# Neighbourhood attention in steps of two heads, and gated-linear units with both head parities together, on one core of a Trainium2

## The chip, the cores and the metric

The kernel runs on one core of a Trainium2 chip. The metric is the device time of one execution in microseconds (us), the median of several runs. The core has five engines, each with its own instruction queue: TensorE (PE, matrix products; PEld is its weight load), VectorE (DVE), ScalarE (ACT), GpSimd (POOL) and SyncE (SP), which issues most DMAs. They wait for each other through semaphores alone.

## What is computed

The reference runs two blocks of two layers each on 512 tokens of width 1024, in fp32. The first block mixes tokens by pooling and latent attention in layer 0 and by neighbourhood attention in layer 1, each followed by cross attention to 256 memory tokens and a squared-ReLU MLP. The second block, on the 512 tokens and 256 context tokens, mixes them by four heads of retention and four heads of gated linear attention (GLA), followed by an MLP. The two parts that matter here:

```python
def neighbourhood_attention(q, k, v, rpb):   # 16 heads of 64, grid of 8 rows x 64 columns
    def one_row(args):
        k_win = k_rows[:, :, col_idx]        # a window of 8 rows x 16 columns for each query
        s = jnp.einsum('bchd,brckhd->bhcrk', q_row, k_win) * scale
        s = s + bias
        p = jax.nn.softmax(s.reshape(B, H, GRID_W, kh * kw), axis=-1)
        return jnp.einsum('bhcrk,brckhd->bchd', p, v_win)

def chunked_gated_linear_attention(q, k, v, log_a, s0, strict):   # chunks of 64 tokens
    def step(s, blk):
        q_dec, k_inv, k_end = qc * exp(cum), kc * exp(-cum), kc * exp(cum_last - cum)
        scores = where(mask, einsum('bhtd,bhsd->bhts', q_dec, k_inv), 0.0)
        o = einsum('bhts,bhsv->bhtv', scores, vc) + einsum('bhtd,bhdv->bhtv', q_dec, s)
        s_new = exp(cum_last[..., 0, :])[..., :, None] * s + einsum('bhsd,bhsv->bhdv', k_end, vc)
```

GLA runs in two directions (d = 0 forward, d = 1 backward), each over 12 chunks (4 of context, 8 of tokens).

## The kernel before

The program is written as one function per engine (`tensor`, `scalar`, `vector`, `gpsimd`, `sync`) that walks through all stages in the order of that engine's queue. A label names the result of an instruction (`then_inc`), and `wait_ge` on the label makes another engine wait for it. All orders are written out by hand. All instructions go through small helpers, so most TensorE rows of the profile carry line 94 (matmul) or 97 (transpose), ScalarE's line 100, and VectorE's lines 107 to 134.

Large projections use split fp32 operands (three products a term, type fp32r). The parts below use plain fp32 operands; each such product stands in the trace as two records, each transpose as one.

**Neighbourhood stage** (TensorE: `neighbour_scores`, `neighbour_transposes`, `neighbour_values`, lines 1060 to 1108; ScalarE: lines 1799 to 1819; VectorE: `divide`, lines 2545 to 2572; GpSimd: line 2967 on). The queries are permuted to blocks of 128 that see 256 keys. For head h the stage has four query blocks q. Two heads share the 128 partitions of O1.Q and O1.K: head h lies on partitions 64 x (h % 2) on, so a score product contracts over 64 rows of the array (form 64*128 in the rows), always the same half within a head. VectorE adds the bias table (O1.BE, made by GpSimd from a DMA of the relative bias and a mask) and takes the least value (line 131), ScalarE takes the exp with its sum, VectorE divides (reciprocal, line 134, and a scaling, line 111), TensorE transposes the 128 x 256 probabilities by halves into banks 2, 3 and 7 in turn, and ScalarE copies a whole head's transposes (two copies of 512 columns, O1.PT). The value products have 64 columns of weights (form 128*64), written to 64 partitions of bank 4 or 5 by the head's parity. ScalarE copies them out ("oh") and VectorE writes the low part ("ol") for the output projection. The loop runs over heads: scores of head h + 1 by blocks, between them the transposes of head h, and after the second block's scores all value products of head h - 1. Scores use banks 0, 1 and 6 in turn.

**GLA units.** `mixed_units` interleaves retention tasks with GLA units. A "work" unit (d, y) stands for a pair of chunks i and a parity par of heads: heads 2j + par, j = 0, 1. There are 12 a direction in layer 0 and 8 in layer 1, 40 in all. On TensorE a unit has `inside` of the next unit (KI by QD: two products that contract over the 64 rows of parity par, form 64*128, 128 columns), then the products of the carried states H.STT with QD (four, 64 rows, 64 columns), then the masked inside scores H.GS with the values H.GV (two full products), all into one bank ("gout"). VectorE's `clip` (line 124) copies the inside scores under a mask into one of two buffers H.GS. The outputs of direction 0 are copied by ScalarE (`first_outputs`), those of direction 1 added by VectorE (`gather`) and multiplied with the gate (`gated`). `gla_banks` hands out banks 4 to 7 in turn, in the order in which the units use them. `states` writes the carried states, state 0 being zeros from a memset.

## Time and profile before

| what | value |
|---|---|
| median of 3 runs | 3515.75 us (3507.23 to 3529.01) |
| the profiled execution, own time | 3525.86 us |
| its span, mean granted TensorE clock | 3524.1 us, 0.979 |
| TensorE busy | 3398.9 us, 96% |
| VectorE, ScalarE, GpSimd busy | 56%, 37%, 7% |
| neighbourhood stage | 975.3 to about 1087 us |
| GLA and retention, layer 0 and layer 1 | about 1960 to 2085, and 2990 to 3090 us |

The profile gives the busy time of each engine, the chain of work that ended last (at each step what released the instruction), groups of instructions by line and shape, and the granted clock of TensorE, where 1.00 is 2.4 GHz and 0.50 is 1.2 GHz. Busy time of TensorE overlaps between neighbouring records, since they are pipelined: how far apart two starts are tells more than a duration.

### The profile page before, as it was taken

Reading aid. Unit: us, or ns where it says so; the run is one execution under the profiler, and the core shown is the slowest. Engines: PE = TensorE matmul, PEld = TensorE weight load, DVE = VectorE, ACT = ScalarE, POOL = GpSimd, SP = SyncE. Lnnn points to the kernel's source line nnn. Section 1 sums busy time; section 2 is a strip of 40 time slices with the busy share of each in tenths; the row PEclk is TensorE's granted clock in tenths of the full one; section 3 lists DMA queues with packets and bytes.
Section 4 is the critical chain, followed back from the end, with each engine's and each line's share of the span. In section 5 each row is a group of like instructions: output and inputs, shape, how many; then the busy total and the mean of one; then the engine's idle time right before and its main releaser. Section 6 shows DMA issues by size and latency. Waiting matters only on the chain.

```text
span 3524.1 us, 41864 instructions
## 1 busy us (share of the span) xinstructions
PE 3398.9 (96%) x17160; PEld 2706.5 (77%) x17160; DVE 1964.9 (56%) x3491; ACT 1320.8 (37%) x2311; POOL 233.9 (7%) x319
## 2 busy tenths in 40 slices
PE   7989999999989999999999889999999999899999
PEld 6747677777867677777898567888888887568887
DVE  6464578886654568887214675333334326664434
ACT  5353434345353444344212443333233313343332
POOL 1200000001041010000000001000001000000000
PEclk9999999999999999999999899999999999899999
DMA  5302145442202135543311021211112321123222
GB/s 177 107 14 84 48 156 167 168 156 90 87 22 70 44 124 171 176 166 118 127 60 49 14 78 41 72 60 60 60 60 67 128 72 42 42 64 102 88 94 72
DMA packets 210181, 317.19 MB, mean 90 GB/s; under 512 B 5377, under 2 KB 154499, under 8 KB 208709
## 3 DMA queue, kind: packets, MB, share of 16 engines
q1 hardware_dynamic: 194180, 243.20, 21.4%
q0 software_dynamic: 15808, 71.31, 5.9%
q8 instruction: 135, 2.21, 0.3%
q14 instruction: 58, 0.47, 0.0%
HBM read 300.76 MB, written 14.59 MB: 89 GB/s over the span
## 4 chain that ended last, share of the span: by engine, by line
PE 84%; DVE 10%; ACT 5%; issue 1%; DMA 1%; ACTq 0%; SPq 0%; DVEq 0%
PE ps L94 83%; ACT t L100 5%; DVE t L115 4%; DVE t L107 3%; PE ps L97 1%; DVE t L111 0%; DVE t L121 0%; DVE t L131 0%; DVE ps L115 0%; DMA t<-in_ada_w 0%; DMA t<-in_w_in 0%; DVE ps L107 0%; DMA t<-in_mem 0%; ACT L100 0%; DVE ps L112 0%
## 5 line engine op out<-in xcount | busy, mean ns | idle before, releaser
L94 PE MATMUL ps<-t,t 128*128 128x512 f32 (+6 forms) x16736 | 3348.5, 365 | 98.0 <-DVE t L115 43.0
L94 PEld LDWEIGHTS ps<-t,t 128*128 128x128 f32 (+3 forms) x16736 | 2657.8, 189 | 761.8 <-issue 150.8
L100 ACT ACTIVATE t<-t 128x1024 fp32r<-128x1024 f32 (+6 forms) x1210 | 846.1, 734 | 1031.3 <-PE ps L94 796.3
L107 DVE TENSOR_TENSOR t<-t,t 128x1024 fp32r<-128x1024 f32 (+4 forms) x799 | 734.2, 953 | 625.3 <-ACT t L100 621.3
L100 ACT ACTIVATE t<-ps 128x512 f32<-128x512 f32 (+6 forms) x552 | 270.7, 517 | 784.4 <-PE ps L94 760.4
L115 DVE SCALAR_TENSOR_TENSOR t<-t,t,t 128x256 f32<-128x256 f32 (+2 forms) x919 | 433.8, 534 | 17.8 <-ACT t L100 11.3
L107 DVE TENSOR_TENSOR t<-ps,t 128x512 f32<-128x512 f32 (+5 forms) x317 | 195.1, 638 | 215.8 <-PE ps L94 147.2
L115 DVE SCALAR_TENSOR_TENSOR t<-ps,t,t 128x512 f32<-128x512 f32 (+2 forms) x252 | 155.0, 662 | 243.5 <-PE ps L94 223.3
L107 POOL TENSOR_TENSOR t<-t,t 128x64 f32<-128x64 f32 (+2 forms) x213 | 150.5, 730 | 1699.3 <-ACT t L100 1695.7
L100 ACT ACTIVATE t<-t,t 128x256 f32<-128x256 f32 (+4 forms) x272 | 144.3, 554 | 214.7 <-DVE t L107 149.7
L118 DVE COPY t<-ps 128x512 f32<-128x512 f32 (+3 forms) x100 | 47.2, 510 | 221.4 <-PE ps L94 208.3
L115 DVE SCALAR_TENSOR_TENSOR t<-ps,t 128x512 f32<-128x512 f32 (+1 forms) x155 | 94.4, 617 | 46.1 <-ACT t L100 24.7
L100 ACT ACTIVATE t<-ps,t 128x256 f32<-128x256 f32 (+3 forms) x92 | 49.5, 546 | 129.4 <-PE ps L94 97.0
L97 PE MATMUL ps<-t,t 128*128 128x128 f32 (+1 forms) x424 | 72.5, 295 | 19.1 <-DMA t<-in_mem 8.1
L97 PEld LDWEIGHTS ps<-t,t 128*128 128x128 f32 (+1 forms) x424 | 51.4, 149 | 47.5 <-issue 14.1
L140 POOL DMA_DIRECT2D t<-in_ada_w x48 | 42.7, 889 | 624.2 <-DVE t L115 624.2
L111 DVE TENSOR_SCALAR t<-t,t 128x256 f32<-128x256 f32 (+3 forms) x173 | 71.7, 418 | 5.9
L121 DVE TENSOR_REDUCE t<-ps 128x1 f32<-128x512 f32 (+1 forms) x64 | 35.4, 553 | 16.2 <-PE ps L94 15.9
L140 POOL DMA_DIRECT2D t<-gates_away x10 | 5.9, 592 | 535.1 <-PE ps L94 506.0
L115 DVE SCALAR_TENSOR_TENSOR t<-t,t,ps 128x128 f32<-128x128 f32 (+1 forms) x96 | 36.2, 380 | 7.0 <-PE ps L94 4.4
L124 DVE COPY_PREDICATED t<-t,ps 128x256 f32<-128x256 int32 x40 | 17.7, 442 | 39.6 <-PE ps L94 39.0
L115 DVE SCALAR_TENSOR_TENSOR ps<-t,ps 128x512 f32<-128x512 f32 (+2 forms) x43 | 27.3, 634 | 19.5 <-ACT t L100 17.5
(36 smaller groups left out, 275.8 us busy)
## 6 DMA issues: line engine op xcount, KB each, us to landing
t<-in_w_ff SPq DMA_DIRECT2D x64, 1024.0 KB, 5.2
t<-in_w_mlp SPq DMA_DIRECT2D x64, 1024.0 KB, 5.3
t<-in_ada_w POOLq DMA_DIRECT2D x48, 1024.0 KB, 5.9
t<-in_w_in SPq DMA_DIRECT2D x30, 1024.0 KB, 5.3
t<-in_w_qkv_o SPq DMA_DIRECT2D x12, 1024.0 KB, 5.1
t<-in_w_mem_kv SPq DMA_DIRECT2D x8, 1024.0 KB, 6.3
t<-in_w_mem_q SPq DMA_DIRECT2D x8, 1024.0 KB, 4.9
t<-in_w_mem_o SPq DMA_DIRECT2D x8, 1024.0 KB, 5.0
```

Of the source, the lines that this page charges most:

```text
L94: return Issued(self, self.e and self.e.matmul(o, l, r, start=start, stop=stop, skip_group_check=True))
L97: return Issued(self, self.e and self.e.transpose(o, i, ident))
L100: return Issued(self, self.e and self.e.activation(o, i, f, **kw))
L107: return Issued(self, self.e and self.e.tensor_tensor(o, a, b, op))
L111: return Issued(self, self.e and self.e.tensor_scalar(o, a, s1, None, op0))
L115: return Issued(self, self.e and self.e.scalar_tensor_tensor(out=o, in0=a, scalar=s1, in1=b, op0=op0, op1=op1))
L118: return Issued(self, self.e and self.e.tensor_copy(o, a))
L121: return Issued(self, self.e and self.e.tensor_reduce(o, a, AX, ALU.max))
L124: return Issued(self, self.e and self.e.copy_predicated(o, mask.bitcast(mybir.dt.int32), a))
L140: return Transfer(self, self.e and self.e.dma_start(dst, src))
```

## The change

**Neighbourhood stage.** The loop runs over 32 steps s; step s is the pair of heads 2j, 2j + 1 with j = s // 4, and block q = s % 4. In each step TensorE issues the scores of both heads, which lie on different row halves, alternately and into different banks (0 and 1, or 6 and 7 in the next step), then the values of step s - 3 and the transposes of step s - 2 (four of them, in one bank, 2 or 3). The value products of both heads go to the two partition halves of one bank (4 or 5 by j), alternately. ScalarE takes two exps, one copy of 512 columns for the four transposes, and copies a pair of heads out at once (128 partitions instead of 64). VectorE has two adds, one reciprocal for both heads, two scalings, and the low part for a pair. O1.SB and O1.PT become four smaller buffers each, O1.BE four buffers instead of two, and the sums lie in a new tile STB (on the space of ST4). GpSimd makes the tables of the heads up to 3 without a wait, and later ones after the last block of the pair before.

**GLA units.** `inside` now issues both parities of a chunk pair, alternating, in even units and two units ahead; `outputs` issues the state products of both parities, alternating, in odd units, followed by the masked products of both. H.GS has four buffers. State 0 is left out: its products are skipped, and the first state is a copy. ScalarE's `first_outputs` and VectorE's `clip`, `gather` and `gated` follow in pairs. In layer 1 pending `states` also run ahead of an "end" unit of retention.

The diff, cut to its core:

```diff
-        for h in range(-1, 17):
-            for q in range(4):
-                if h + 1 < 16:
-                    neighbour_scores(h + 1, q)
-                if h > 0 and q == 1:
-                    neighbour_values(h - 1)
-                if 0 <= h < 16 and q > 0:
-                    neighbour_transposes(h, q - 1)
-            if 0 <= h < 16:
-                neighbour_transposes(h, 3)
+        for s in range(35):
+            if s < 32:
+                neighbour_scores(s)
+            if s >= 3:
+                neighbour_values(s - 3)
+            if 2 <= s < 34:
+                neighbour_transposes(s - 2)
...
+        def neighbour_scores(s):
+            j, q = s // 4, s % 4
...
+            windows = [(0, 256, 128 * q)] if q < 3 else [(0, 128, 384), (128, 128, 0)]
+            for x, (o0, n, t0) in enumerate(windows):
+                for a in range(2):
+                    bk, r0 = score_banks[s % 2][a], 64 * a
+                    if x == 0:
+                        opening(bk)
+                    ins = pe.matmul(P[bk][:, o0:o0 + n], O1.Q[r0:r0 + 64, j, 128 * q:128 * q + 128], O1.K[r0:r0 + 64, j, t0:t0 + n],
+                                    x == 0, x == len(windows) - 1)
...
+        def neighbour_values(s):
...
+            pe.wait_ge("pt", "na", s)
+            for c0, t0, n in [(0, 128 * q + 64, 128)] if q < 3 else [(0, 448, 64), (64, 0, 64)]:
+                for z in range(2):
+                    for a in range(2):
+                        h = 2 * j + a
+                        ins = pe.matmul(P[bk][64 * a:64 * a + 64, t0:t0 + n], O1.V[:, (q + z) % 4, 64 * h:64 * h + 64],
+                                        O1.PT[s % 4][:, 2 * a + z, c0:c0 + n], q == 0 and z == 0, t0 == 0 and z == 1)
...
         def inside(d, y):
-            i, par = work[d][y]
-            b0, bk = 64 * par, gb["inside", d, y]
-            opening(bk)
+            i = work[d][y][0]
+            bks = [gb["inside", d, y + par] for par in range(2)]
+            for bk in bks:
+                opening(bk)
             for j in range(2):
                 pe.wait_ge("qd", l, d, j)
                 pe.wait_ge("ki", l, d, j)
-                ins = pe.matmul(P[bk][:, 128 * j:128 * j + 128], H.KI[b0:b0 + 64, j, 128 * i:128 * i + 128],
-                                H.QD[b0:b0 + 64, j, 128 * i:128 * i + 128], True, True)
+                for par in range(2):
+                    b0 = 64 * par
+                    ins = pe.matmul(P[bks[par]][:, 128 * j:128 * j + 128], H.KI[b0:b0 + 64, j, 128 * i:128 * i + 128],
+                                    H.QD[b0:b0 + 64, j, 128 * i:128 * i + 128], True, True)
...
+        def outputs(d, y):
+            i, order = work[d][y][0], chunk_order(d)
+            obs = [gb["gout", d, y + par] for par in range(2)]
+            for ob in obs:
+                opening(ob)
+            carried = [(j, c, order.index(c)) for j in range(2) for c in two(i) if order.index(c) > 0]
+            for x, (j, c, n) in enumerate(carried):
+                pe.wait_ge("state", l, d, j, n)
+                for par in range(2):
+                    b0, o0 = 64 * par, 128 * j + 64 * (c % 2)
+                    pe.matmul(P[obs[par]][:, o0:o0 + 64], H.STT[b0:b0 + 64, j, n - 1, :], H.QD[b0:b0 + 64, j, 64 * c:64 * c + 64],
+                              x == 0, False)
+            for par in range(2):
+                pe.wait_ge("gmask", l, d, i, par)
+                for j in range(2):
+                    h = 2 * j + par
+                    ins = pe.matmul(P[obs[par]][:, 128 * j:128 * j + 128], H.GV[:, i, 128 * h:128 * h + 128],
+                                    H.GS[(y + par) % 4][:, j, :], False, j == 1)
...
-                if y + 1 < len(work[d]):
-                    inside(d, y + 1)
...
+                if y % 2 == 0 and y + 2 < len(work[d]):
+                    inside(d, y + 2)
+                if y % 2 == 1:
+                    outputs(d, y - 1)
...
                 for h in range(16):
                     pl.wait_ge("bias_in", h)
-                    if h >= 2:
-                        pl.wait_ge("sfree", "na", h - 2, 3)
+                    if h >= 4:
+                        pl.wait_ge("sfree", "na", 4 * (h // 2) - 5, h % 2)
```

How TensorE's queue stands in the neighbourhood stage. A row is output <- operands and the shape of the output; ps is a bank, t7 the constants with the identity. Before, t69 and t68 are O1.K and O1.Q, t71 and t72 are O1.SB, t73 and t74 are O1.PT, t70 is O1.V. The rows from one head's values on:

```order
L94 MATMUL ps4<-t73_121,t70_118 64x128 x6
L94 MATMUL ps4<-t73_121,t70_118 64x64 x4
L97 MATMUL ps7<-t7_55,t72_120 128x128
L97 MATMUL ps2<-t7_55,t72_120 128x128
L94 MATMUL ps1<-t69_117,t68_116 128x256
L97 MATMUL ps7<-t7_55,t72_120 128x128
L97 MATMUL ps2<-t7_55,t72_120 128x128
L94 MATMUL ps6<-t69_117,t68_116 128x128 x2
L97 MATMUL ps7<-t7_55,t72_120 128x128
L97 MATMUL ps2<-t7_55,t72_120 128x128
L97 MATMUL ps7<-t7_55,t72_120 128x128
L97 MATMUL ps2<-t7_55,t72_120 128x128
```

After (O1.K t70, O1.Q t69, O1.V t71, O1.SB t72 to t75, O1.PT t76 to t79), two steps and the scores of a third:

```order
L94 MATMUL ps0<-t70_118,t69_117 128x256
L94 MATMUL ps1<-t70_118,t69_117 128x256
L94 MATMUL ps4<-t77_125,t71_119 64x128 x4
L97 MATMUL ps2<-t7_55,t74_122 128x128 x4
L94 MATMUL ps6<-t70_118,t69_117 128x256
L94 MATMUL ps7<-t70_118,t69_117 128x256
L94 MATMUL ps4<-t78_126,t71_119 64x128 x4
L97 MATMUL ps3<-t7_55,t75_123 128x128 x4
L94 MATMUL ps0<-t70_118,t69_117 128x256
L94 MATMUL ps1<-t70_118,t69_117 128x256
```

One head's ten value products in a block, once a head, have become four in each step, two heads in turn; scores come in pairs for two banks, and the four transposes of a step stand together, where they came in twos between the scores.

How the queue stands at two GLA units of layer 0, direction 0. Before, t119 is H.KI, t118 H.QD, t121 H.STT, t131 and t132 H.GS, t113 H.GV, t115 and t114 the gate of the other direction, t104 and t105 retention keys and queries, t14 its decayed scores, t123 its values:

```order
L94 MATMUL ps4<-t118_166,t119_167 128x128 x2
L94 MATMUL ps5<-t118_166,t121_169 128x64 x4
L94 MATMUL ps5<-t132_180,t113_161 128x128 x2
L94 MATMUL ps6<-t115_163,t114_162 128x256
L94 MATMUL ps7<-t118_166,t119_167 128x128 x2
L94 MATMUL ps4<-t118_166,t121_169 128x64 x4
L94 MATMUL ps4<-t131_179,t113_161 128x128 x2
L94 MATMUL ps0<-t104_152,t105_153 128x512
```

After (H.QD t125, H.KI t126, H.STT t128, H.GS t129, t139, t140 and t141, H.GV t120, gate t122 and t121, retention t111, t112, t14 and t131), from the inside products of one pair to the first state products of the pair before:

```order
L94 MATMUL ps4<-t125_173,t126_174 128x128
L94 MATMUL ps5<-t125_173,t126_174 128x128
L94 MATMUL ps4<-t125_173,t126_174 128x128
L94 MATMUL ps5<-t125_173,t126_174 128x128
L94 MATMUL ps0<-t111_159,t112_160 128x512
L94 MATMUL ps3<-t14_62,t131_179 128x256
L94 MATMUL ps6<-t122_170,t121_169 128x256
L94 MATMUL ps7<-t125_173,t128_176 128x64
L94 MATMUL ps4<-t125_173,t128_176 128x64
L94 MATMUL ps7<-t125_173,t128_176 128x64
L94 MATMUL ps4<-t125_173,t128_176 128x64
```

The inside products no longer stand directly ahead of state products of the other half: they alternate among themselves, and a retention task and a gate product lie between them and the outputs. The second output of a pair (ps4) uses the bank of the inside product issued just before.

## Rows read from the trace of the kernel before

**Rows 1.** The page: the chain that ended last, by engine, and VectorE's clips

```profile
PE 84%; DVE 10%; ACT 5%; issue 1%; DMA 1%; ACTq 0%; SPq 0%; DVEq 0%
...
L124 DVE COPY_PREDICATED t<-t,ps 128x256 f32<-128x256 int32 x40 | 17.7, 442 | 39.6 <-PE ps L94 39.0
```

**Rows 2.** Windows: stretch, length, busy us of PE, PEld, DVE, ACT, POOL, clock, DMA

```profile
975.30:1087.00 111.70, 98.74 (x611) 74.54 (x612) 64.57 (x271) 61.96 (x176) 47.20 (x126) 0.91 0.09 25
1003.30:1060.60 57.30, 50.87 (x346) 37.62 (x345) 36.61 (x153) 35.01 (x100) 30.49 (x81) 1.00 0.14 40
979.40:989.60 10.20, 10.20 (x39) 7.38 (x39) 5.51 (x25) 5.32 (x17) 6.26 (x18) 0.50 0.09 27
1960.00:2085.00 125.00, 108.71 (x730) 69.39 (x728) 87.50 (x202) 50.08 (x115) 9.28 (x12) 0.92 0.14 48
2990.00:3090.00 100.00, 89.58 (x498) 56.91 (x490) 63.49 (x139) 32.75 (x71) 6.85 (x8) 0.80 0.15 49
```

**Rows 3.** The chain that ended last, one head: start, length, what

```profile
1007.60 1.97 PE ps L94 x20
...
1009.60 0.60 ACT t L100
...
1010.22 0.69 DVE t L107
...
1012.85 1.09 ACT t L100 x2
```

**Rows 4.** Timeline of TensorE, one head: start, length, group, idle before

```profile
1014.08 1.96 PE L94 MATMUL ps<-t,t 128*64 128x128 f32 x20 [0.87 <-ACT t L100]
1015.97 0.44 PE L97 MATMUL ps<-t,t 128*128 128x128 f32 x2
1016.33 0.70 PE L94 MATMUL ps<-t,t 64*128 64x256 f32 x2
1016.96 0.44 PE L97 MATMUL ps<-t,t 128*128 128x128 f32 x2
...
1017.97 0.66 PE L97 MATMUL ps<-t,t 128*128 128x128 f32 x4
1018.55 1.13 PE L94 MATMUL ps<-t,t 64*128 64x256 f32 x4
```

**Rows 5.** Groups by shape, TensorE, 201.3 to 202.9 us (first attention stage)

```profile
L94 PE MATMUL ps<-t,t 128*64 128x512 f32 x8 | 1.9, 605 | 0.0
```

**Rows 6.** Groups by shape, TensorE, 2011.80 to 2012.85 us (one GLA unit)

```profile
L94 PE MATMUL ps<-t,t 64*128 64x64 f32 x8 | 1.1, 278 | 0.0
L94 PE MATMUL ps<-t,t 64*128 64x128 f32 x4 | 0.7, 297 | 0.0
```

**Rows 7.** Timeline of VectorE in the neighbourhood stage

```profile
1017.30 0.41 DVE L131 CUSTOM_DVE_ANT_0 t<-ps,t 128x256 f32<-128x256 f32 x1
...
1017.64 0.15 DVE L134 RECIPROCAL t<-t 128x1 f32<-128x1 f32 x1
1017.83 0.35 DVE L111 TENSOR_SCALAR t<-t,t 128x256 f32<-128x256 f32 x1
1018.10 0.42 DVE L131 CUSTOM_DVE_ANT_0 t<-ps,t 128x256 f32<-128x256 f32 x1
```

**Rows 8.** Timeline of ScalarE, the same stretch

```profile
1018.56 0.51 ACT L100 ACTIVATE t<-t,t 128x256 f32<-128x256 f32 x1 [0.20 <-DVE t L131]
...
1019.06 1.06 ACT L100 ACTIVATE t<-ps 128x512 f32<-128x512 f32 x2
```

**Rows 9.** Timeline of TensorE and window of a slow stretch

```profile
1064.75 3.58 PE L94 MATMUL ps<-t,t 128*64 128x128 f32 x20 [0.87 <-ACT t L100]
...
1064.80:1068.20 3.40, 3.40 (x20) 3.39 (x20) 0.61 (x2) 0.78 (x4) 1.67 (x7) 0.51 0.02 5
```

**Rows 10.** The chain, by line: 1960 to 2085, then 2990 to 3090

```profile
by line: PE ps L94 48.9%; DVE t L115 21.4%; DVE t L107 11.6%; ACT t L100 9.8%; issue 2.9%; DVE t L124 2.4%; DVE t L111 2.2%; DVE t L137 0.5%; DVE t L118 0.3%; DVEq L91 0.1%
by line: PE ps L94 69.6%; DVE t L115 15.3%; DVE t L107 6.8%; ACT t L100 6.7%; issue 1.2%; DVE t L137 0.3%; DVE t L118 0.2%; DVEq L91 0.0%
```

232 lines of the change are left out of this document (107 added, 125 removed).

## The prediction

> **What bounds the kernel now.** I read the page first: the chain that ended last and the costliest groups [rows 1]. TensorE carries 84% of the chain; VectorE has 10%, ScalarE 5%. So time is won only where TensorE's own instructions shorten or a wait of TensorE goes. Then the stages that the change touches, by windows [rows 2]: the neighbourhood stage (975.3 to 1087) and the gated-linear stages of the two layers (1960 to 2085, 2990 to 3090). All three have TensorE below full: 98.7 of 111.7, 108.7 of 125, 89.6 of 100 us, at granted clocks of 0.91, 0.92 and 0.80.
>
> Inside the neighbourhood stage the nine heads from 1003.3 to 1060.6 run at a clock of 1.00, at 57.3 / 9 = 6.37 us a head [rows 2]. The chain of one head [rows 3] shows why: the value products (1.97 us), the copy out (0.60), the low part on VectorE (0.69), adds and exps, the two transposed copies (1.09, to 1013.94), and the values of the next head at 1014.08, 0.14 us later [rows 4]. It is a ring through three engines: TensorE has its groups to get through, and waits before each values group (0.87 us at 1014.08, [rows 4]). All its score products use 64 rows of the array and all its value products 64 columns, and one head's products lie on the same half, so they go one after the other: 20 records of values take 1.96 us [rows 4]. (A product of fp32 operands stands as two records, a transpose as one.)
>
> **Can two halves run together?** Rows of this kernel say so. In the first attention stage, products of 64 columns alternate between column halves: 8 records of 512 columns in 1.9 us [rows 5], where in line they would need 3.4: a record of 128 columns follows the one before it at some 0.11 (the 20 value records of [rows 4] are twelve of 128 and eight of 64 columns in 1.89 us), one of 512 at four times that. For row halves: in a gated-linear unit four records of 128 columns (KI by QD, one half) stand ahead of eight of 64 columns (state by QD, other half), and the twelve fit in 1.1 us [rows 6], which is what the eight need alone (0.11 each and 0.2 to leave the mode). So this overlap partly exists already, and the gated-linear units have less to win than their order suggests.
>
> A rule speaks against that. The Trainium skill, "TensorE: Matmul & The Clock Gate", Part 3 (the mechanism), has matmuls start and end in strict program order, and weight loads pass a running matmul only where the row group differs. By it the value products on two column halves would gain little, and the unit of [rows 6] would need 4 x 0.11 more. The trace does not agree with either, so the sum goes by the rows; what is left of the rule is the third rival.
>
> **The neighbourhood stage, step by step.** Before: the 111.7 us of the window [rows 2], of which the last 0.5 belongs to the next stage: 111.2. After: 32 steps of two heads and one query block. On TensorE each step is scores, values of three steps ago, transposes of two steps ago.
>
> TensorE, from the starts of groups [rows 4]: two score records of one head take 0.63 up to the next group (1016.33 to 1016.96); with the second head on the other half still 0.63. Four transposes 0.58 (1017.97 to 1018.55). The values: 20 records take 1.89 (1014.08 to 1015.97), the four pairs of a step some 4 x 0.11 + 0.11 = 0.55. Sum 1.76 a step. These figures contain the three changes of array mode.
>
> ScalarE: two exps of 0.51, a copy of 0.53 [rows 8], a quarter of the 0.60 for the copy out [rows 3]: 1.70. VectorE: two adds at 0.34 apart, one reciprocal 0.19 (before two), two scalings 0.27 [rows 7], a quarter of the low part's 0.69 [rows 3]: 1.57; with whole durations (0.42, 0.15, 0.35) 1.9. GpSimd: 30.5 us busy for nine tables [rows 2], 3.4 a head, 6.8 a pair of heads against four steps; it now may begin as soon as the pair before has freed the table at its last block, and has five steps.
>
> No engine binds alone, the ring does. Over two steps: from the end of a transposed copy to TensorE 0.14; values 0.55; transposes 0.58; scores finished 0.70; handed to VectorE 0.04; add until exp 0.46 (1018.10 in [rows 7], 1018.56 in [rows 8]); two exps until the copy 1.02; the copy 0.58 (two that overlap a little take 1.06). Sum 4.07, so 2.04 a step, and the low part once in four steps pushes an add by 0.2: 2.10. I take 2.15 for what meets by chance. What hides the rest is thin: 0.4 us of TensorE, 0.45 of ScalarE.
>
> Stage after: 1.2 to the first exp, 31 x 2.15 = 66.7, the last exps 1.0, and the tail of two copies, transposes and values 5.3: 74.2 us. Then the clock. At 1.2 GHz the 20 value records take 3.58 instead of 1.96 [rows 9]; the 1.3 us that a step streams become 2.6, so the step is TensorE's at 3.06, or 0.9 longer: 30% of slow time is lost. The 10.2 us at 0.50 after the start [rows 2] stay (TensorE waits there on the first heads as before): 3.1. TensorE stands idle 0.4 of each 2.15 us, about twice the share of the heads (0.87 of 6.37 at most), so I add three more spells of the shortest kind seen, 3.4 us at 0.51 [rows 9], 1.0 each. Total 80.3: **31 us less**. Bounds: no spell and 2.04 a step, 71 us (40 less); slow half of the time or more, 95 (16 less).
>
> **The gated-linear units.** There are 24 and 16, 20 pairs. Before, a unit's half-array part is 1.06 us [rows 6] and 0.09 to enter the mode, 2.3 a pair. After: KI by QD of both parities together, four pairs of records 4 x 0.11 + 0.2 + 0.09 = 0.73; state by QD, eight pairs 8 x 0.11 + 0.2 + 0.09 = 1.17. Sum 1.9: 0.4 less a pair, 8 us if all lay on the chain. But TensorE carries 49% of the chain in the first layer's stage and 70% in the second [rows 10] and most units stand in TensorE's parts of it; I count 14 pairs, 5.6. The four products with a zero state in each direction go as well, 4 pairs of records at 0.11, 1.8 for the four directions, 1 of it on the chain. Against it: both outputs of the last pair of a direction now come together, so VectorE's (or ScalarE's) sums and gates of the earlier one are late by some 0.4 + 0.4, four times: 3. Net **4 less**. The clips are as many as before (40 at 0.44 [rows 1]); four buffers are cleared in each direction instead of two: 8 more memsets of a clip's size, at most 8 x 0.44 = 3.5, of which TensorE's work hides nearly all where it has the chain.
>
> From this execution's own 3525.86 us (span 3524.1) 35 less is 3491; it lies 10 above the median of the three runs, and the difference is carried to the median: 3515.75 - 35 = 3481.
>
> **Rivals.**
>
> 1. The clock. It stood at 1.2 GHz at the start of this stage, after TensorE had waited for the first heads, and again at 1064.8, after a wait of 0.87 us [rows 2, 9]. For: TensorE's idle share doubles. Against: a slow step leaves TensorE no idle time, and in all of the places that I looked at the clock came back under such work. Alternating 1.2 and 2.4 costs 60 x 0.5 x 0.3 = 9, worse phases 16: 3490 to 3497. Chance 0.18.
> 2. Outputs that wait on a bank. Two KI products of the next pair stand ahead of the outputs of this one on four rotating banks, and the second output of a pair takes the bank of a KI product; TensorE then waits for VectorE's clip of a block that it doesn't need yet, and behind it stand the retention products. For: VectorE is on the chain in the first layer [rows 10]. Against: a retention task and a gate lie between. Two clips of 0.44 [rows 1] a pair: 20 x 0.88 = 18, 4 becomes -14: 3499. Chance 0.13.
> 3. The halves do not run together in the new order, since each half's two records stand together and the banks or weight loads meet. Place: every half-array group. Price: scores +0.43 and values +0.44 a step make TensorE 2.63 a step, 15 us of the 31 gone; and what overlaps today in the units is lost: a pair takes 8 x 0.11 + 16 x 0.11 + 0.5 = 3.1 against 2.3, 20 x 0.8 = 16 more, with the 3 for late outputs. 3515.75 - 16 + 16 + 3 = **3519, slower than before**. It decides from the point where less than half of the records overlap. Chance 0.04. If only the column halves fail, 0.44 a step lengthens the ring by 0.2: 7 us, 3488; inside the range.
> 4. The bias tables. GpSimd's 6.8 us a pair would bind if a table landed late: its next load starts when the one two heads back is used. That decides at 8.6 - 3.4 = 5.2 us from issue to landing; today GpSimd is ready with a table before it is wanted, and five steps are 10.8 us. 3485 to 3500. Chance 0.03.
>
> **How the numbers follow.** Forecast 0.62, rivals 0.18, 0.13, 0.04, 0.03. A measurement of this kernel tells about 1%, 35 us, from no change, and the forecast lies on that bound: its own range is 3468 to 3491, a little over half of its weight beyond the bound (0.35), and the first rival's bound (fewer slow spells than I added) adds 0.07 to that side. Faster by over 1%: 0.42. Slower by over 1% needs 35 us the other way, more than rival 3 gives alone: 0.03. Within: 0.55. Range 3466 to 3504, down to all spells and overlaps going well and up through rivals 1 and 2.
>
> **What would show it.** In the new profile: (a) scores and values as pairs of records a few ns apart, steps of 2.0 to 2.3 us in a stretch at clock 1.00, the stage done in 76 to 86 us; (b) the chain there shared by TensorE, ScalarE and VectorE, with ScalarE's wait before exps short and TensorE's wait before values 0.2 to 0.5; (c) granted clock of the stage 0.8 to 0.95; lower tells rival 1; (d) the gated-linear stages shorter by 0 to 4 us each, no wait of TensorE for the clip (COPY_PREDICATED); such waits of 0.5 or more tell rival 2; (e) steps of 2.6 us and records of the two halves one after the other tell rival 3. The prediction is wrong if the stage takes over 92 or under 70 us, or the gated-linear stages move by over 10.

## The result, and the profile after

| | before | after |
|---|---|---|
| median (4 executions each) | 3517.98 us | 3459.68 us (3456.16 to 3464.38) |
| ratio, 95% interval | | 0.9828 (0.9803 to 0.9853) |
| the profiled execution, span | 3524.1 us | 3454.3 us |
| neighbourhood stage, at 1.2 GHz in it | 110.9 us, 20 | 68.4 us, 0 |
| layer 0 gated-linear stage, at 1.2 GHz in it | 153.9 us, 23 | 143.9 us, 27 |
| layer 1 gated-linear stage, at 1.2 GHz in it | 136.6 us, 41 | 123.5 us, 17 |

The change makes the kernel 1.7% faster, 58 us by the medians. The forecast was 35 us less and the range ended at 3466, so the time lies 6 us below the range. Stage lengths here and below go from start to start in the trace: the neighbourhood stage from its first score product to its last value product, a gated-linear stage from its first product over 33 rows (the gates) to its last half-array product. The four stretches between and around them differ by 0.7 to 2.7 us each. The two profiled executions lie 70 us apart and the medians 58, because the one before was 8 us above its median and the one after the fastest of its four.

The page after, chain and clips, beside [rows 1]:

```profile
PE 84%; DVE 10%; ACT 5%; issue 1%; DMA 0%; ACTq 0%; SPq 0%; DVEq 0%
...
L124 DVE COPY_PREDICATED t<-t,ps 128x256 f32<-128x256 int32 x40 | 16.3, 439 | 19.6 <-PE ps L94 19.0
```

The shares of the whole did not move: the program is still TensorE's. In the neighbourhood stage they did (ScalarE had 26% of the chain there before and VectorE's L131 9%, against 55% for TensorE's two lines):

```profile
by line: ACT t L100 42.9%; PE ps L94 25.2%; PE ps L97 11.2%; issue 9.0%; DVE t L131 6.0%; DVE t L111 3.0%; DVE t L107 2.1%; DVE t L134 0.6%; DVEq L91 0.0%
```

The windows of the changed stages, with the columns of [rows 2]; the second is a steady stretch of the neighbourhood stage:

```profile
974.10:1042.70 68.60, 60.74 (x609) 39.63 (x609) 52.91 (x231) 53.61 (x167) 38.10 (x108) 1.00 0.13 37
990.00:1033.00 43.00, 39.90 (x401) 25.91 (x400) 35.58 (x156) 35.78 (x113) 29.83 (x86) 1.00 0.18 51
1905.00:2030.00 125.00, 108.99 (x740) 68.08 (x738) 90.93 (x210) 53.60 (x126) 11.24 (x14) 0.89 0.13 45
2932.00:3024.00 92.00, 76.52 (x518) 48.92 (x510) 65.01 (x143) 32.65 (x71) 6.84 (x8) 0.91 0.16 55
```

The granted clock of the neighbourhood stage went from 0.91 to 1.00: no stretch at 1.2 GHz is left, not even the 10.2 us at its start. TensorE's idle share in the steady stretch fell from 11% (50.87 of 57.3 busy, [rows 2]) to 7% (39.90 of 43.0), where I had said that it would double. What TensorE did there, by shape, first before (975.3 to 1087), then after (974.1 to 1042.7):

```profile
L94 PE MATMUL ps<-t,t 64*128 64x256 f32 x96 | 30.6, 428 | 1.5 <-ACT t L100 1.0 <-DVE t L131 0.5
L94 PE MATMUL ps<-t,t 128*64 128x128 f32 x192 | 29.1, 311 | 12.4 <-ACT t L100 12.4
L97 PE MATMUL ps<-t,t 128*128 128x128 f32 x128 | 25.0, 302 | 0.0
```

```profile
L97 PE MATMUL ps<-t,t 128*128 128x128 f32 x128 | 21.0, 287 | 0.7 <-DVE t L111 0.7
L94 PE MATMUL ps<-t,t 64*128 64x256 f32 x96 | 16.9, 426 | 1.2 <-ACT t L100 1.0 <-DVE t L131 0.2
L94 PE MATMUL ps<-t,t 128*64 128x128 f32 x192 | 15.8, 285 | 5.8 <-ACT t L100 5.1
```

The same 96 score records and 192 value records cover 16.9 instead of 30.6 and 15.8 instead of 29.1 us, while one record lasts about as long as before (426 for 428 ns, 285 for 311): two run at a time. By the windows, 38.0 of the 43.1 us won are TensorE's busy time (98.74 to 60.74) and 5.1 its idle time. The clock can be at most some 10 of them, since 20 us stood at half of the full clock. TensorE and ScalarE in two steady steps (beside [rows 4, 8]):

```profile
1010.37 0.66 PE L97 MATMUL ps<-t,t 128*128 128x128 f32 x4
1010.96 0.71 PE L94 MATMUL ps<-t,t 64*128 64x128 f32 x8
1011.85 0.66 PE L94 MATMUL ps<-t,t 128*64 128x128 f32 x8 [0.17 <-ACT t L100]
1012.43 0.66 PE L97 MATMUL ps<-t,t 128*128 128x128 f32 x4
1013.02 1.46 PE L94 MATMUL ps<-t,t 64*128 64x256 f32 x12
```

```profile
1010.22 0.51 ACT L100 ACTIVATE t<-t,t 128x256 f32<-128x256 f32 x1 [0.51 <-DVE t L131]
...
1011.22 1.06 ACT L100 ACTIVATE t<-ps 128x512 f32<-128x512 f32 x2
1012.19 0.51 ACT L100 ACTIVATE t<-t,t 128x256 f32<-128x256 f32 x1
...
1014.33 0.51 ACT L100 ACTIVATE t<-t,t 128x256 f32<-128x256 f32 x1 [0.57 <-DVE t L131]
```

Steps follow at 1.97 and 2.14 us (first exps at 1010.22, 1012.19, 1014.33); from the fifth on their mean is 2.03.

In the gated-linear stage of layer 0 the shape to look at is the product of state and QD (64 rows, 64 columns). Before (1960 to 2085), then after (1905 to 2030):

```profile
L94 PE MATMUL ps<-t,t 64*128 64x64 f32 x192 | 28.2, 290 | 1.0 <-DVE t L115 1.0
L94 PE MATMUL ps<-t,t 64*128 64x128 f32 x96 | 16.1, 310 | 6.2 <-DVE t L115 6.2
```

```profile
L94 PE MATMUL ps<-t,t 64*128 64x64 f32 x174 | 14.1, 307 | 1.4 <-DVE t L115 1.4
L94 PE MATMUL ps<-t,t 64*128 64x128 f32 x96 | 10.3, 342 | 4.9 <-DVE t L115 4.9
```

In layer 1 (2990 to 3090 before, 2932 to 3024 after) large products take part as well:

```profile
L94 PE MATMUL ps<-t,t 128*128 128x512 f32 x74 | 42.4, 705 | 0.2 <-DVE t L107 0.2
L94 PE MATMUL ps<-t,t 64*128 64x64 f32 x120 | 21.6, 336 | 1.6 <-DVE t L115 1.6
```

```profile
L94 PE MATMUL ps<-t,t 128*128 128x512 f32 x86 | 38.3, 573 | 2.4 <-DVE t L107 2.4
...
L94 PE MATMUL ps<-t,t 64*128 64x64 f32 x128 | 11.1, 325 | 5.3 <-DVE t L115 5.0 <-DVE t L124 0.3
```

More of the 512-column records (86 for 74) take less time (38.3 for 42.4): one took 705 ns before and takes 573 now. That is the clock (0.80 to 0.91), not the order. But part of this is not the change's doing: e1, which has the old gated-linear units, shows 24 us at 1.2 GHz in layer 1 (129.0 us long) and 33 in layer 0 (159.4). How the slow spells fall on the two layers moves from kernel to kernel. Both stages together take 288 to 301 us in the three kernels with the old units (e1, before, e6), 267 us after, and 266 to 272 in the others with the change in these units. The last row also answers rival 2 in part: TensorE waits for a clip (L124) for 0.3 us in all. Its weight loads wait for clips five times, 3.0 us in the whole run and 0.8 at most, which they did not before.

### The profile page after: what moved, and what is told of

The parts are those of the page before. It is cut to its first block, busy times and chain, and to the rows that moved or that the text cites. A ratio compares the mean times of both kernels' runs of the same rounds, so it can differ in the third digit from the quotient of the medians.

```text
span 3454.3 us, 41772 instructions
## 1 busy us (share of the span) xinstructions
PE 3334.1 (97%) x17144; PEld 2652.8 (77%) x17144; DVE 1950.4 (56%) x3451; ACT 1312.4 (38%) x2303; POOL 233.2 (7%) x319
## 4 chain that ended last, share of the span: by engine, by line
PE 84%; DVE 10%; ACT 5%; issue 1%; DMA 0%; ACTq 0%; SPq 0%; DVEq 0%
PE ps L94 83%; ACT t L100 5%; DVE t L115 4%; DVE t L107 3%; PE ps L97 1%; DVE t L111 0%; DVE t L121 0%; DVE ps L115 0%; DVE t L124 0%; DMA t<-in_w_in 0%; DVE ps L107 0%; DMA t<-in_mem 0%; ACT L100 0%; DVE t L131 0%; DVE t L118 0%
## 5 line engine op out<-in xcount | busy, mean ns | idle before, releaser
L94 PE MATMUL ps<-t,t 128*128 128x512 f32 (+5 forms) x16720 | 3285.6, 364 | 93.0 <-DVE t L115 42.3
L94 PEld LDWEIGHTS ps<-t,t 128*128 128x128 f32 (+2 forms) x16720 | 2604.2, 188 | 749.1 <-issue 144.4
L100 ACT ACTIVATE t<-t,t 128x256 f32<-128x256 f32 (+4 forms) x272 | 143.9, 552 | 202.3 <-DVE t L107 149.0
L118 DVE COPY t<-ps 128x512 f32<-128x512 f32 (+4 forms) x108 | 49.3, 492 | 220.1 <-PE ps L94 207.3
L100 ACT ACTIVATE t<-ps,t,t 128x512 f32<-128x512 f32 x32 | 24.9, 779 | 29.1 <-DVE t L107 29.0
```

The lines of the kernel that those rows point to most:

```text
L94: return Issued(self, self.e and self.e.matmul(o, l, r, start=start, stop=stop, skip_group_check=True))
L100: return Issued(self, self.e and self.e.activation(o, i, f, **kw))
L118: return Issued(self, self.e and self.e.tensor_copy(o, a))
```

## The experiments

Two theories ran against each other. Theory 1: what counts is that half-array products of opposite halves stand next to each other in TensorE's queue; that brings the overlap and keeps the clock up. Theory 2 is, in each, the cheapest other cause. The kernels were timed on several chips, each beside the kernel before, so across chips the ratios are what to compare.

| run | kernel | median us | ratio to before (95%) | neighbourhood stage (at 1.2 GHz) |
|---|---|---|---|---|
| e1 | neighbourhood part alone | 3474.27 | 0.9875 (0.9858, 0.9891) | 68.4 (0) |
| e2 | gated-linear part alone | 3499.17 | 0.9947 (0.9931, 0.9962) | 111.0 (20) |
| e3 | no early states | 3456.42 | 0.9827 (0.9810, 0.9844) | 68.4 (0) |
| e4 | neighbourhood step head by head | 3559.46 | 1.0116 (1.0100, 1.0131) | 169.5 (165) |
| e5 | e4 and a full-array product a step | 3503.74 | 0.9933 (0.9918, 0.9948) | 110.3 (0) |
| e6 | before and full-array products | 3529.85 | 1.0009 (0.9996, 1.0022) | 113.9 (3) |
| e7 | products by head, adjacent | 3459.72 | 0.9814 (0.9801, 0.9828) | 70.8 (0) |
| e8 | gated-linear outputs parity by parity | 3484.59 | 0.9886 (0.9869, 0.9903) | 68.4 (0) |
| e9 | inside products parity by parity | 3455.12 | 0.9809 (0.9790, 0.9828) | 68.4 (0) |
| e10 | after and full-array products in the units | 3459.75 | 0.9821 (0.9800, 0.9841) | 68.4 (0) |
| e11 | e8 and the same products | 3482.39 | 0.9886 (0.9865, 0.9906) | 68.4 (0) |
| e12 | scores of the two heads apart | 3525.29 | 1.0009 (0.9998, 1.0021) | 137.3 (133) |
| e13 | e12 and a full-array product a step | 3490.46 | 0.9911 (0.9894, 0.9929) | 97.8 (0) |
| e14 | transposes ahead of the values | 3451.41 | 0.9810 (0.9789, 0.9830) | 61.2 (0) |
| e15 | the changed kernel, beside e16 | 3457.48 | 0.9820 (0.9805, 0.9835) | 68.4 (0) |
| e16 | e14 again | 3454.24 | 0.9813 (0.9799, 0.9827) | 61.1 (0) |

**e1 and e2: the two parts.** Each kernel is before with one of the two halves of the diff; no line of its own.

> Before, with the neighbourhood part of the change alone. Theory A (the forecast's shares): the stage loses 31 us, the whole kernel 31. Theory B (read from the new trace): the stage goes from 111.2 to 68.6 us, because a step takes 1.97 us instead of 2.15 and the clock stays at 1.00; the kernel is 40 to 44 us faster than before, and the rest of the 58 belongs to the gated-linear part. Theory C (the clock in the stage before was chance): 34 to 38.

> Before, with the gated-linear part of the change alone. Theory A (forecast): 4 us faster. Theory B: the two gated-linear stages lose 10 and 13 us as in the new trace, 20 to 23 faster. Theory C (half of that was the clock of one execution): 12 to 18 faster.

The neighbourhood part gives 44 us, the gated-linear part 19 (ratios 0.9875 and 0.9947): 63 together, beside 60 for both (0.9828). The forecast had 31 and 4. The slow clock in the stage before was no accident of one execution: e2's profile, with the old neighbourhood stage, has the same four spells at the same places in the stage, 20 us in sum.

**e3: the early states of layer 1.**

```diff
-                while l == 1 and collected:
-                    states(*collected.pop())
```

> The changed kernel without the two lines that run pending states ahead of an end unit of retention in layer 1. Theory 1 (these lines are worth a wait that the forecast did not price: in layer 1 of the kernel before, the products of k_end and v were held up for 4.3 us by VectorE): 3 to 6 us slower than the changed kernel. Theory 2 (the gain of the gated-linear stages is alternation and clock): within 1 us.

No effect that can be measured (0.9827 for 0.9828).

**e4 and e5: the neighbourhood step head by head.** The step becomes scores of head 0, values of head 0, scores of head 1, values of head 1, transposes. e5 adds to each step one product of the identity with constants, 256 columns, written to columns that nothing reads.

```diff
+            for heads in ((0,), (1,)):
+                if s < 32:
+                    neighbour_scores(s, heads)
+                if s >= 3:
+                    neighbour_values(s - 3, heads)
...
+                pe.matmul(P[score_banks[s % 2][0]][:, 256:512], cst("ident"), CST[:, 0:256], True, True)
```

> The changed kernel with the neighbourhood products of the two heads kept apart: in each step scores of head 0, values of head 0, scores of head 1, values of head 1, transposes. Nothing overlaps, and each step has two more changes of array mode. Theory 1 (alternation carries the gain): a step of TensorE grows from 1.76 by 0.43 + 0.44 + 2 x 0.17 to some 3.0 us, the stage by 32 x 1.0 = 30 us or more, so that most of the stage's gain goes. Theory 2 (steps of two heads with fewer waits carry it, the overlap is beside the ring): the stage grows by under 12 us.

> The kernel of e4 (neighbourhood products of the two heads apart) with one product more in each step: identity by 256 constant columns, all 128 rows and columns, into an unused part of a score bank; nothing reads it. It adds 0.43 us of TensorE work a step. In e4 the clock was 0.50 for all 165 us of the stage while TensorE was 100% busy. Theory 1 (lone half-array products do not bring the clock back, full ones do): clock near 1.00, stage 105 to 120 us, some 50 us faster than e4 although it does more. Theory 2 (the clock has nothing to do with it, the products take that long): the stage grows to 180 or more.

Windows of e4 (990 to 1100) and of e5 (990 to 1060), then TensorE's timeline of e5:

```profile
990.00:1100.00 110.00, 110.00 (x385) 69.92 (x384) 35.22 (x151) 36.69 (x107) 31.00 (x90) 0.50 0.07 20
```

```profile
990.00:1060.00 70.00, 70.00 (x429) 46.22 (x428) 35.54 (x151) 34.52 (x108) 30.92 (x90) 1.00 0.12 33
```

```profile
1021.42 0.66 PE L97 MATMUL ps<-t,t 128*128 128x128 f32 x4
1021.92 0.60 PE L94 MATMUL ps<-t 128*128 128x256 f32 x2
1022.44 2.51 PE L94 MATMUL ps<-t,t 64*128 64x128 f32 x16
1024.88 0.66 PE L97 MATMUL ps<-t,t 128*128 128x128 f32 x4
1025.37 0.60 PE L94 MATMUL ps<-t 128*128 128x256 f32 x2
```

Without pairs the changed kernel is slower than before: I had expected 30 us or more, and the stage takes 101 more. The clock falls 5 us into the stage (976.8), after waits of 1.02, 0.20 and 0.74 us, which the changed kernel has too, and stays at 1.2 GHz for the other 165 us, while TensorE is busy 98% of the time (100% in the window). More work on the whole array ends that: e5 does all that e4 does and 0.52 us a step on top (1021.92 to 1022.44), and its stage is 59 us shorter, at 1.00 throughout. A step of e5 is 3.45 us (1021.92 to 1025.37), 2.93 without the addition, against 2.03: overlap, with two changes of mode less, is worth 0.9 x 31 = 28 of the 101 us that e4 lost, the clock the other 73.

**e6: the same addition to the kernel before**, 128 columns a score block.

```diff
             opening(bk)
+            pe.matmul(P[bk][:, 384:512], cst("ident"), CST[:, 0:128], True, True)
```

> The kernel before with one product more ahead of each block of neighbourhood scores: identity by 128 constant columns on the whole array, 0.22 us, 64 times; nothing reads it. The stage before has 20 us at half clock and TensorE waits 0.6 to 0.9 us a head. Theory 1 (the idle or half-filled array costs the clock): slow time 0 to 10 us, the 14 us of added work lie half in the waits, stage 105 to 114 us against 111. Theory 2 (clock falls here by the schedule, whatever TensorE does): slow time stays near 20, stage 115 to 125.

It takes the slow clock away (20 to 3 us) and costs more than that gives: 113.9 for 110.9 us. The clock is no free gain in the old order; it is one in the new order because no work is added.

**e7: products by head, but adjacent.** Loops over x and a (scores), and over z and a (values), with the head outermost.

> The changed kernel with the neighbourhood products of a step ordered by head instead of alternating: all value products of head 0 and then all of head 1, and the same for the two-part scores, still next to each other in one mode. Theory 1 (TensorE works through the products of different halves out of order, as the rows of the gated-linear unit before suggested): no change, stage 68 to 70 us, within 2 us in all. Theory 2 (only neighbours in the order overlap): values grow by 3/4 of 0.44 a step, stage 75 to 80, and the clock may fall.

TensorE's timeline of e7:

```profile
1012.22 0.66 PE L97 MATMUL ps<-t,t 128*128 128x128 f32 x4
1012.81 0.70 PE L94 MATMUL ps<-t,t 64*128 64x256 f32 x4
1013.77 0.66 PE L94 MATMUL ps<-t,t 128*64 128x128 f32 x8 [0.26 <-ACT t L100]
1014.36 0.44 PE L97 MATMUL ps<-t,t 128*128 128x128 f32 x2
```

Four score records in 0.70 and eight value records in 0.59 us (1013.77 to 1014.36), as in the changed kernel, though one head's four value records stand ahead of the other's four. So the strict alternation isn't needed. But it was not free either: the stage takes 70.8 us, and in all other profiles with pairs and the groups in this order it takes 68.4. In every fourth step the values are in two parts, and eight records of one head (64 columns each) stand ahead of eight of the other. These sixteen take 0.90 us up to the next group (1015.70 to 1016.60), 0.62 in the changed kernel. Their starts show why: five records follow each other alone, 0.06 to 0.11 us apart, the next starts 6 ns after the fifth, five more start within 0.17 us of it, and the last five stand alone again.

That the other half's records start ahead of their turn can be seen where their shapes tell them apart, in the kernel before. In one of its units the queue holds four records of KI by QD (64x128) and behind them eight of state by QD (64x64, other half). In the first 0.1 us (2011.80 to 2011.90) the trace has of that unit one record of each, 13 ns apart:

```profile
L94 PE MATMUL ps<-t,t 64*128 64x128 f32 x1 | 0.4, 373 | 0.0
L94 PE MATMUL ps<-t,t 64*128 64x64 f32 x1 | 0.3, 320 | 0.0
```

So the fifth record of the queue starts right after the first, ahead of three that stand before it; in e7 the ninth starts right after the fifth, if the two streams are its two heads. Both pass three waiting records, which would be why eight ahead of eight lose and four ahead of four do not.

**e8: the units' outputs parity by parity** (state products and masked products of one parity, then of the other).

```diff
-            for x, (j, c, n) in enumerate(carried):
-                pe.wait_ge("state", l, d, j, n)
-                for par in range(2):
+            for par in range(2):
+                for x, (j, c, n) in enumerate(carried):
+                    pe.wait_ge("state", l, d, j, n)
```

> The changed kernel with the outputs of a gated-linear pair taken parity by parity: state products of one parity, its masked products, then those of the other. Two more changes of mode a pair, no overlap among state products. Theory 1 (alternation carries the gain of the gated-linear part): a pair grows by 0.9 + 0.2 us on TensorE, 14 to 20 of the 20 pairs on the chain, and the clock falls more: 15 to 30 us slower than the changed kernel. Theory 2 (pairing and its looser waits carry it): under 8 us slower.

The state products of e8 in layer 0 (1905 to 2040):

```profile
L94 PE MATMUL ps<-t,t 64*128 64x64 f32 x176 | 28.0, 305 | 1.4 <-DVE t L115 1.4
```

28.0 us, as before the change (28.2), and twice the 14.1 of the changed kernel. The run is 25 us slower than e7 on the same chip (ratio 0.9886 for 0.9814), which is more than the whole gain of e2.

**e9: inside products parity by parity**, the loops over j and par of `inside` exchanged.

> The changed kernel with the two inside products of one parity ahead of the two of the other; the outputs alternate as in the change. Theory 1 (halves overlap only where neighbours in the queue alternate): 20 pairs lose 4 records of 0.11 us, 0.44 each, 8.8 us, of which the two thirds to nine tenths on the chain are 6 to 9 us: 3466 to 3470 us. Theory 2 (TensorE takes products of the other half past waiting ones over a short distance, as seen with the scores and values ordered by head): two products of a half are close enough, no change, 3458 to 3462 us.

No loss (3455.12 us, even below the 3458 to 3462 expected): two products of one half are near enough to the other two, as in e7's short groups.

**e10 and e11: full-array products ahead of each pair of outputs.**

```diff
+            pe.matmul(P[obs[0]][:, 256:384], cst("ident"), CST[:, 0:128], True, True)
             carried = [(j, c, order.index(c)) for j in range(2) for c in two(i) if order.index(c) > 0]
```

> The changed kernel with one more full-array product (identity by constants, 128 columns, two records) ahead of each pair of outputs in the gated-linear stages, written to columns that nothing reads. Theory 1 (lone half-array products and waits let the clock fall; full-array work brings it back): the 44 us at 1.2 GHz in the two stages become under 20, worth some 0.3 to 0.4 each, 8 to 10 us, against 20 x 0.15 = 3 us of added work: 3450 to 3455 us, faster than the changed kernel. Theory 2 (the clock falls by TensorE's waits alone, which the filler doesn't remove): slow time as before and 3 us more: 3462 to 3464 us.

> The kernel with the gated-linear outputs parity by parity (e8) and the same added full-array product ahead of each pair of outputs. Beside e8 it splits the 25 us that e8 lost into clock and overlap. Theory 1 (20 pairs x 8 records x 0.11 = 18 us of overlap, and 24 us more at 1.2 GHz worth 7): the slow time falls below 30 us and the run lies at 3475 to 3481 us, 18 to 22 above e10. Theory 2 (the loss was mostly clock): it comes within 10 us of e10.

Both theories missed. In e10 layer 0 has 17 us at 1.2 GHz instead of 27 and takes 142.7 us instead of 143.9, layer 1 20 us and 126.8 instead of 123.5: the slow time stays at 38 us, where I had expected under 20, and the run is not faster. In e11 it is 51 us, where I had expected under 30, and e11 stands to before as e8 does (0.9886 both). So one full-array product of 128 columns a pair does little for the clock here (38 us for 44), where 256 columns a step ended all of the slow time in the neighbourhood stage. e11 against e10 still tells something of e8: in layer 0 the slow time is alike (14 and 17 us) and e11 takes 152.8, 10.1 more, which is lost overlap and two more changes of mode a pair. In layer 1 it takes 14.8 more, with 17 us more at 1.2 GHz.

**e12 and e13: only the row halves apart.** The step becomes scores of head 0, transposes, scores of head 1, values of both heads; e13 adds the full-array product of e5.

```diff
-                neighbour_scores(s)
+                neighbour_scores(s, (0,))
+            if 2 <= s < 34:
+                neighbour_transposes(s - 2)
+            if s < 32:
+                neighbour_scores(s, (1,))
             if s >= 3:
                 neighbour_values(s - 3)
-            if 2 <= s < 34:
-                neighbour_transposes(s - 2)
```

> The changed kernel with the neighbourhood step ordered scores of one head, four transposes, scores of the other head, values of both heads (still alternating). Only the row halves lose their overlap (two score records of 256 columns, some 0.43 us a step) and the step changes the array's mode once more (0.1 to 0.2); the column halves keep theirs, and two full-array groups of transposes a step no longer stand together with anything. Theory 1 (each pair of halves is worth its records, and full-array transposes in every step keep the clock at 2.4 GHz): TensorE 1.75 + 0.5 = 2.3 us a step against 1.97, the stage 10 us longer, clock 1.00: 3466 to 3472 us. Theory 2 (the clock also falls where scores of one head stand alone): 1.2 GHz for a third or more of the stage, 20 us or more longer, above 3478 us.

> The kernel of e12 (scores of the two heads apart) with a full-array product of 256 columns (identity by constants) added in each of the 32 steps, written to columns of a score bank that nothing reads. Theory 1 (the 69 us that e12 lost are mostly the clock, and full-array work brings it back): granted clock 1.00 through the stage, a step of 2.3 us of TensorE plus 0.4 of the added product, about 2.7, the stage 85 to 92 us, the run 3477 to 3485 us. Theory 2 (the step order itself is slow, by banks or waits): the stage stays above 110 us, the run above 3500 us.

Windows of e12 (990 to 1100) and e13 (990 to 1060), and TensorE's timeline of e13:

```profile
990.00:1100.00 110.00, 110.00 (x473) 67.34 (x474) 41.30 (x181) 42.21 (x131) 31.75 (x90) 0.50 0.07 21
```

```profile
990.00:1060.00 70.00, 70.00 (x484) 42.72 (x478) 39.39 (x167) 39.08 (x121) 30.69 (x90) 1.00 0.11 32
```

```profile
1020.97 0.70 PE L94 MATMUL ps<-t 128*128 128x256 f32 x2
1021.60 0.70 PE L94 MATMUL ps<-t,t 64*128 64x256 f32 x2
1022.22 0.66 PE L97 MATMUL ps<-t,t 128*128 128x128 f32 x4
1022.81 1.28 PE L94 MATMUL ps<-t,t 64*128 64x256 f32 x10
1024.02 0.70 PE L94 MATMUL ps<-t 128*128 128x256 f32 x2
```

This was the surprise of the study. I expected 10 us, since two records a step lose their partner; it cost 69, and the whole gain of the change was gone (ratio 1.0009). e13 splits it: a step of 3.05 us (1020.97 to 1024.02) with 0.63 of addition is 2.42, so the lost overlap and the extra change of mode cost 0.39 a step, 12 us, close to what I expected; e12's steps are 4.39 us, so the clock costs 1.97 a step, 61 us. (The two make 73 over 31 steps; the first three steps are shorter, so the stage lost 69.) e13's own stage, 97.8 us, is above the 85 to 92 expected, because the added product took 0.63 us and not 0.4. Here too the clock fell early, 4 us into the stage, after waits of 1.02, 0.20 and 1.09 us, and did not come back: pairs of value products alone were not enough to bring TensorE back to 2.4 GHz.

**e14, e15 and e16: transposes ahead of the values.** All pairs stay; only the order of the groups in a step changes.

```diff
-            if s >= 3:
-                neighbour_values(s - 3)
             if 2 <= s < 34:
                 neighbour_transposes(s - 2)
+            if s >= 3:
+                neighbour_values(s - 3)
```

> The changed kernel with the transposes of a step ahead of its values (scores, transposes, values). All halves still come in pairs. Theory 1 (pairs in the queue are what keep the clock and the overlap): clock 1.00, steps of 1.95 to 2.1 us, 3456 to 3464 us; since ScalarE's copy starts 0.45 us earlier in a step it could be a little faster, at best 2 us. Theory 2 (the place of the transposes behind the values matters to the clock): a stage with slow spells, above 3470 us.

> The changed kernel itself, as a control beside e16 on the same chip. Expected 3455 to 3462 us; neighbourhood stage 68.4 us at clock 1.00, steps of 2.04 us in the mean.

> The kernel of e14 beside the changed kernel on one chip. Theory 1 (the ring transposes, copy, values sets the step, and with the transposes ahead of the values ScalarE's copy has 0.55 us more before the values need it): the stage 61 us again, and the whole 5 to 8 us less than e15. Theory 2 (e14 was a good draw; steps are set by ScalarE's 1.7 us and chance): within 2 us of e15.

The window of e16's stage:

```profile
972.00:1034.00 62.00, 60.24 (x610) 40.22 (x609) 53.72 (x233) 54.05 (x170) 38.68 (x108) 1.00 0.14 41
```

In both runs the stage takes 61 us instead of 68.4, with a mean step of 1.85 instead of 2.03 us. On one chip the medians are 3454.24 and 3457.48, 3 us apart, and the ratios' intervals overlap (0.9813 and 0.9820); e14 on another chip had 3451.41. Of the two theories of e16, 5 to 8 us less and within 2, neither is met by 3 us. The 7 us are plain in the stage, where I had expected 2 at best; in the whole they are near what the other stages' clock scatters by (layer 1 had 27 us at 1.2 GHz in e14 and e15, 17 in e16 and in the profile after). It has the shortest stage of all versions and is 1.9% faster than before; in the whole it can't be told from e9 (0.9809) or the changed kernel.

## Why the prediction was wrong, step by step

The direction was right, and so was the overlap of the halves. What failed was the clock, which I had tied to TensorE's idle time and which is the larger error in both stages, if barely so in the first, and two sizes: the step of 2.15 us and the 14 pairs on the chain.

- **Halves run together** (from [rows 5] and [rows 6]): right. The rule of the Trainium skill, "TensorE: Matmul & The Clock Gate", Part 3 (the mechanism), has weight loads pass a running matmul only where the row group differs, which would have left the value products, on two column halves, nearly without overlap. The trace does not agree: 192 value records cover 15.8 us instead of 29.1. The same part has matmuls start and end in strict program order, which would have left e7's order with little overlap. The trace does not agree with this either: e7's eight records take 0.59 us (0.58 in the changed kernel), and in the kernel before a record starts ahead of three that stand before it. Rival 3 fell.
- **"I take 2.15" a step**: the ring's 2.04 was right and my additions were not. 31 steps took 61.1 us from first exp to first exp, not 66.7. The steady mean of 2.03 already holds the low part, for which I added 0.06, and chance, for which I added 0.05; the first three steps, which have no values yet, took 1.0 to 1.5. That is 5.6 us. e14 fits the ring as I described it: with the transposes 0.6 us earlier in a step it shortens to 1.85. That 2.04 and 2.03 agree so closely is in part luck: the first leaves the low part out, the second holds it.
- **"The 10.2 us at 0.50 after the start stay", and "three more spells"**: wrong, and the main miss here, 6.1 us in the forecast where there were none. I had tied the clock to TensorE's idle time, of which I said that its share doubles (by my own numbers it went from 11 to 14% to 19%; measured, it fell). The changed kernel has the waits at the start of the stage and no fall. e4 and e12 show TensorE busy over 98% at 1.2 GHz for 165 and 133 us, and e5 and e13 at 2.4 GHz with a full-array product more in each step. So in the new loop it is setting the halves apart that costs the clock. What remains open is the kernel before: all its half-array products stand alone, and still it ran at 1.00 in 90 of 111 us and came back from each of its four spells. 80.3 forecast, 68.4 measured: 5.6 and 6.1 are the difference.
- **"The slow step leaves TensorE no idle time, and the clock came back"**, my argument against rival 1: a wrong reason for a right chance. e12 has no idle time and the clock did not come back.
- **The gated-linear units, "0.4 less a pair"**: right. In single pairs of chunks at clock 1.00 the half-array part went from 2.10 to 1.69 us. **"I count 14 pairs" on the chain**: wrong. Summed from start to start over both stages, half-array products with 64 rows of weights take 39.5 us instead of 51.6. These 12.1 us all came off, where I had 6.6; TensorE's idle time grew by 1.7 us, not 3. (Among the 12.1 are the zero states, for which I had 1 on the chain, counting four directions. They exist in two: layer 0 went from 192 to 176 records of state by QD, layer 1 kept its 128, since it has outputs for token chunks alone and the context chunks come first in both directions.) The share of the chain said where the chain ran, not how much shortening would pass through.
- **The clock of the gated-linear stages**: a term that I didn't have. Other products of TensorE take 10.7 us less in layer 1, where 41 us at 1.2 GHz became 17 (one 512-column record 705 to 573 ns). Layer 0 has no such gain (23 and 27 us) and is 10.0 us shorter, 5.6 of it in half-array products and 2.7 in idle time. That the change itself brought layer 1's gain is not shown: in e1, with the old units, the other products take 6.4 us less there too. In both layers together 57 to 89 us are at 1.2 GHz with the old units (e1, before, e6) and 39 to 51 with the new ones in the order of the change. Both stages together: 23.1 us less in the profiles, 19 in e2, 4 forecast.
- **Signs named ahead**: steps of 2.0 to 2.3 came true; a stage of 76 to 86 us and a clock of 0.8 to 0.95 did not; the stage under 70 and gated-linear stages that move by over 10 were what I had said would prove the prediction wrong, and they did. The chain there is shared as named (TensorE's two lines 36%, ScalarE 43%). ScalarE's waits before exps are not short: 17 of them in the steady 43 us, 7.8 us in all. TensorE's waits before values are 0.05 to 0.27, mostly below the 0.2 to 0.5 named. Of rival 2 there is a trace, five waits of weight loads for clips, two of them in layer 0 (1.4 us), and no loss that shows; rival 4 did not show: no DMA or GpSimd among what TensorE and ScalarE waited for in the steady stretch.

The 35 us of the forecast against 60 (by the ratio) come from 12 in the neighbourhood stage and 13 to 19 in the gated-linear ones.

## What to carry to other kernels

Where products use half of the array, put those of opposite halves next to each other in the queue, all groups of a loop and not only the largest: the overlap is worth its records. In the new loop, taking the halves apart cost two to five times as much again through the clock (73 for 28 us in e4, 61 for 12 in e12); against the kernel before, which stood at 1.2 GHz for only 20 us of the stage, the clock gave the change at most 10 us there. A stretch at 1.2 GHz need not end because TensorE is busy; look at the shapes in it, and try one full-array product more in each step as a test (it told clock from overlap in e5 and e13, and did little in the gated-linear units). Then order the groups so that the one which another engine must copy comes first (e14: 7 us less in the stage).

## What the runs showed of the hardware that was not expected

- TensorE can stay at 1.2 GHz for a whole stage while it is busy over 98% of the time: 165 us in e4, 133 us in e12. With added full-array products the same stages ran at 1.00 (e5, e13), 59 and 39 us shorter with more work. The kernel before, with lone half-array products too, came back to 1.00 each time; why is open.
- Pairs need not alternate record by record: four records of one half ahead of four of the other took 0.59 us for eight (e7), eight ahead of eight took 0.90 for sixteen instead of 0.62. A record of the other half starts ahead of three that stand before it in the queue (state by QD in the kernel before, 13 ns after the first record).
- Setting four of the sixteen records of a step apart from their partners (e12) cost as much as the whole change had gained, five sixths of it through the clock.
